# Rotary positions of the attention heads: tables with the column gains in them, quarters exchanged by transfers, and the head's sum and low part on VectorE

## The reference, cut to what matters

```python
def rope_rotate(x, ang):
    m = ang.shape[-1]
    x1, x2 = x[..., :m], x[..., m:]
    c = jnp.cos(ang)[:, None, :]
    s = jnp.sin(ang)[:, None, :]
    return jnp.concatenate([x1 * c - x2 * s, x2 * c + x1 * s], axis=-1)
...
    q = rms_norm(q.reshape(b_, s_, ATTN_HEADS, HEAD_DIM), qn_g)
    k = rms_norm(k.reshape(b_, s_, KV_HEADS, HEAD_DIM), kn_g)
    q = apply_axial_rope(q, ang_row, ang_col)
    k = apply_axial_rope(k, ang_row, ang_col)
...
        sc = jnp.einsum('bqkgd,bskd->bkgqs', qblk, k).astype(jnp.float32) * scale
        pr = jax.nn.softmax(sc, axis=-1).astype(v.dtype)
        return jnp.einsum('bkgqs,bskd->bqkgd', pr, v)
```

## Time and profile before

| what | value |
|---|---|
| median of three runs | 1665.84 us |
| the profiled execution | 1665.42 us, of which its span is 1663.6 us |
| granted TensorE clock, mean of the span | 0.993 |
| TensorE matmul busy | 1618.1 us, 97% |
| VectorE, ScalarE, GpSimd busy | 64%, 40%, 6% |
| stretch of the units above | about 851 to 1089 us of the span |

### The profile page before, as it was taken

The page is one execution under the profiler, slowest core; times in us unless marked ns, Lnnn a source line. Parts: engine busy times, 40 slices in busy tenths (PEclk is TensorE's granted clock), DMA queues, the critical chain, the costliest instruction groups (busy, mean ns, idle before and its releaser), DMA issues.

```text
span 1663.6 us, 23794 instructions
## 1 busy us (share of the span) xinstructions
PE 1618.1 (97%) x9484; PEld 1566.3 (94%) x9484; DVE 1057.5 (64%) x1628; ACT 668.9 (40%) x1073; POOL 102.2 (6%) x59
## 2 busy tenths in 40 slices
PE   5999999999999999999999999999999999999999
PEld 5999889989999999999999888788999999999998
DVE  6432665676776577477653666668767747756764
ACT  4333224453343244144332666655424414423431
POOL 4000200000000000000122322100000000000000
PEclk7999999999999999999999999999999999999999
DMA  4122002221222222212211100022122221221222
GB/s 135 51 64 63 26 14 69 59 76 50 78 76 67 61 77 78 75 51 70 83 58 39 38 21 20 9 80 64 55 73 77 73 77 54 70 80 55 77 71 81
DMA packets 193629, 103.85 MB, mean 62 GB/s; under 512 B 3792, under 2 KB 191184, under 8 KB 193520
## 3 DMA queue, kind: packets, MB, share of 16 engines
q1 hardware_dynamic: 193040, 101.20, 21.5%
q0 software_dynamic: 144, 0.79, 0.1%
q10 hardware_dynamic: 336, 0.35, 0.1%
HBM read 99.18 MB, written 3.15 MB: 62 GB/s over the span
## 4 chain that ended last, share of the span: by engine, by line
PE 92%; DVE 4%; ACT 1%; issue 1%; DMA 0%; POOL 0%; SPq 0%; ACTq 0%; DVEq 0%; POOLq 0%
PE unit_ps L536 15%; PE unit_ps L537 14%; PE unit_ps L538 14%; PE unit_ps L819 13%; PE unit_ps L817 13%; PE unit_ps L818 13%; PE unit_ps L995 2%; PE misc_ps L682 1%; PE misc_ps L536 1%; PE misc_ps L538 1%; PE misc_ps L952 1%; PE misc_ps L537 1%; PE misc_ps L963 1%; PE unit_ps L710 1%; PE misc_ps L668 1%
## 5 line engine op out<-in xcount | busy, mean ns | idle before, releaser
L817 PE MATMUL unit_ps<-h_pair,w_hi 128*128 128x384 f32 x1232 | 412.2, 335 | 3.1 <-ACT t L1297 3.0
L819 PE MATMUL unit_ps<-h_pair,w_lo 128*128 128x384 f32 x1232 | 411.6, 334 | 0.0
L818 PE MATMUL unit_ps<-h_pair,w_hi 128*128 128x384 f32 x1232 | 411.6, 334 | 0.0
L536 PE MATMUL unit_ps<-pair_b,w_hi 128*128 128x384 f32 x960 | 323.3, 337 | 6.5 <-DVE w_lo L1429 5.0
L538 PE MATMUL unit_ps<-pair_b,w_lo 128*128 128x384 f32 x960 | 320.9, 334 | 0.0
L537 PE MATMUL unit_ps<-pair_b,w_hi 128*128 128x384 f32 x960 | 320.8, 334 | 0.0
L817 PEld LDWEIGHTS unit_ps<-h_pair,w_hi 128*128 128x128 f32 x1232 | 231.2, 188 | 4.2 <-ACT t L1297 3.6
L818 PEld LDWEIGHTS unit_ps<-h_pair,w_hi 128*128 128x128 f32 x1232 | 231.3, 188 | 0.0
L819 PEld LDWEIGHTS unit_ps<-h_pair,w_lo 128*128 128x128 f32 x1232 | 231.2, 188 | 0.0
L536 PEld LDWEIGHTS unit_ps<-pair_b,w_hi 128*128 128x128 f32 x960 | 180.2, 188 | 8.9 <-DVE w_lo L1429 6.3
L537 PEld LDWEIGHTS unit_ps<-pair_b,w_hi 128*128 128x128 f32 x960 | 180.3, 188 | 0.6
(11 more groups left out here) (241 smaller groups left out, 2109.3 us busy)
## 6 DMA issues: line engine op xcount, KB each, us to landing
w_raw<-in_w_gate SPq DMA_DIRECT2D x22, 512.0 KB, 3.9
w_raw<-in_w_up SPq DMA_DIRECT2D x22, 512.0 KB, 5.2
w_raw_more<-in_w_gate SPq DMA_DIRECT2D x22, 512.0 KB, 3.9
w_raw_more<-in_w_up SPq DMA_DIRECT2D x22, 512.0 KB, 5.2
w_raw<-in_w_down SPq DMA_DIRECT2D x24, 384.0 KB, 3.5
w_raw_more<-in_w_down SPq DMA_DIRECT2D x24, 384.0 KB, 3.6
w_raw<-in_ab_w_in SPq DMA_DIRECT2D x17, 512.0 KB, 3.9
w_raw<-in_c_w_in SPq DMA_DIRECT2D x12, 512.0 KB, 3.8
```

The lines of the kernel that those rows point to most:

```text
L536: pe.matmul(out, w_hi, m_hi, start=start, stop=False)
L817: pe.matmul(out, hi, m_hi, start=starts and k == 0, stop=False, skip_group_check=True)
L818: pe.matmul(out, hi, m_lo, start=False, stop=False, skip_group_check=True)
L819: last = pe.matmul(out, lo, m_hi, start=False, stop=k == HK - 1, skip_group_check=True)
```

## The change

A head's exchange of quarters no longer runs on TensorE. The sine table carries the signs, and ScalarE scales both tables by the gains in place (`gained_ropes`, line 1351 before goes): once for the keys, and, after GpSimd has loaded the tables a second time, once for the queries, with the gains of the sine table exchanged as the quarters are. VectorE evacuates a head straight into T[2] or T[3]; ScalarE squares from there; SyncE issues four transfers per head inside the on-chip memory, 32 partitions by 768 columns each, that write T[0] as the head with its quarters exchanged (`turn_head`, placed in SyncE's order ahead of the load of the unit four later). VectorE then does T[0] times the sine table, T[4] plus T[0] (slot at+4 for a query, at+6 for a key), and the low part (`head_lo`, slot at+9). GpSimd is left with the product by the cosines. The high part moves to slot at+7. The factor 128 to the power -1/2 goes into `head_root`, and the small instruction of line 1887 goes. The table of constants is a fourth shorter, `columns` three columns longer.

```diff
-    _put(_at + (4 if _kind == "q" else 5), "turn", _i, 0)
-    _put(_at + (6 if _kind == "q" else 5), "turn", _i, 1)
-    _put(_at + 8, "split", _i)
+    if _kind == "k":
+        _put(_at + 5, "broadcast", _i)
+    _put(_at + (6 if _kind == "k" else 4), "turn", _i)
+    _put(_at + 7, "split", _i)
+    _put(_at + 9, "low", _i)
...
+            def turn_head(i):
+                sp.wait_ge(unit_read, reads(BASE["c"] + UNIT_OF[i]))
+                if i:
+                    sp.wait_ge(qk_sum, i)
+                for quarter in range(4):
+                    to, of = quarter * HD // 4, (quarter ^ 1) * HD // 4
+                    sp.dma_start(T[0][to:to + HD // 4, :], T[2 + i % 2][of:of + HD // 4, :]).then_inc(turn_landed, 16)
...
+                        if n - TURN_LOADS in UNIT_OF:
+                            turn_head(UNIT_OF.index(n - TURN_LOADS))
...
             def head_sums(i):
                 pe.wait_ge(qk_sq, i + 1)
-                if i:
-                    pe.wait_ge(rot_read, 2 * i)
+                pe.wait_ge(root_done, CHAIN["qk"] + i)
...
-            def turn(i, half):
-                pe.wait_ge(qk_gain, i + 1)
...
-                pe.matmul(misc_ps[:, bank, 0:HALF], rot, T[2 + i % 2][:, half * HALF:(half + 1) * HALF],
-                          start=True, stop=True).then_inc(rot_done, 1)
...
             def head_evacuate(i, n):
                 if i:
-                    act.wait_ge(qk_sum, i)
-                act.activation(T[1][:, :], T[0][:, :], ACT.Square).then_inc(qk_sq, 1)
-                if i >= 2:
-                    act.wait_ge(rot_done, 2 * (i - 1))
-                    act.wait_ge(qk_cos, i - 1)
-                act.activation(T[2 + i % 2][:, :], T[0][:, :], ACT.Copy, scale=cols[:, col:col + 1]).then_inc(qk_gain, 1)
+                    act.wait_ge(colsum_done, CHAIN["qk"] + i)
+                act.activation(T[1][:, :], T[2 + i % 2][:, :], ACT.Square).then_inc(qk_sq, 1)
...
+            def gained_ropes(kind, turn):
+                act.wait_ge(rope_landed, 16 * turn)
+                for part, col in enumerate((COL[kind + "n"], COL[kind + "n_turned"])):
+                    act.activation(ropes[:, part, :], ropes[:, part, :], ACT.Copy,
+                                   scale=cols[:, col:col + 1]).then_inc(rope_gained, 1)
...
+            gained_ropes("k", 1)
             for slot in range(SLOTS):
+                if slot == 8 * (UNIT_OF[KVH] + 1) - 4:
+                    gained_ropes("q", 2)
...
-                    done = dve.tensor_tensor(T[0][:, half * HALF:(half + 1) * HALF], ps, rstd[:, half, :], ALU.mult)
+                    i = UNIT_OF.index(j)
+                    if i >= 2:
+                        dve.wait_ge(qk_sq, i - 1)
+                        dve.wait_ge(qk_cos, i - 1)
+                        dve.wait_ge(turn_landed, 4 * 16 * (i - 1))
+                    done = dve.tensor_tensor(T[2 + i % 2][:, half * HALF:(half + 1) * HALF], ps, rstd[:, half, :], ALU.mult)
...
-                dve.tensor_tensor(T[1][:, tokens], misc_ps[:, bank, 0:HALF], ropes[:, 1, tokens], ALU.mult).then_inc(rot_read, 1)
+                dve.wait_ge(turn_landed, 4 * 16 * (i + 1))
+                dve.wait_ge(rope_gained, 2 if QK[i][1] == "k" else 4)
+                dve.tensor_tensor(T[0][:, :], T[0][:, :], ropes[:, 1, :], ALU.mult).then_inc(turn_scaled, 1)
+                dve.wait_ge(turn_scaled, i + 1)
+                dve.wait_ge(qk_cos, i + 1)
+                dve.tensor_tensor(T[4][:, :], T[4][:, :], T[0][:, :], ALU.add).then_inc(qk_sum, 1)
...
+            def head_lo(i):
+                dve.wait_ge(qk_hi, i + 1)
+                pair = kpair[:, QK[i][2]] if QK[i][1] == "k" else pairB[:, QK[i][2]]
+                dve.tensor_tensor(pair[:, 1, :], T[4][:, :], pair[:, 0, :].bitcast(F32), ALU.subtract).then_inc(qk_lo, 1)
...
+            load_ropes()
+            for i, (n, kind, _) in enumerate(QK):
+                if i == KVH:
+                    pool.wait_ge(qk_sum, KVH)
+                    load_ropes()
+                pool.wait_ge(unit_read, reads(BASE["c"] + n))
+                pool.wait_ge(rope_gained, 2 if kind == "k" else 4)
                 if i:
                     pool.wait_ge(qk_lo, i)
+                    pool.wait_ge(qk_hi, i)
                 pool.tensor_tensor(T[4][:, :], T[2 + i % 2][:, :], ropes[:, 0, :], ALU.mult).then_inc(qk_cos, 1)
-                pool.wait_ge(qk_cos, i + 1)
-                pool.wait_ge(rot_read, 2 * i + 2)
-                pool.tensor_tensor(T[4][:, :], T[4][:, :], T[1][:, :], ALU.add).then_inc(qk_sum, 1)
-                pool.wait_ge(qk_hi, i + 1)
-                pool.tensor_tensor(pair[:, 1, :], T[4][:, :], pair[:, 0, :].bitcast(F32), ALU.subtract).then_inc(qk_lo, 1)
```

More of the change, by code:

```diff
@@ L203 @@
 UNIT_OF = [n for n, _, _ in QK]
+TURN_LOADS = 4
 LAG = 3
@@ L999, in between @@
             def between(slot):
-                for what, i, *half in PLAN.get(slot, ()):
+                for what, i in PLAN.get(slot, ()):
                     if what == "sums":
                         head_sums(i)
[L1003 to L1006, removed]
+                    elif what == "broadcast":
+                        broadcast(CHAIN["qk"] + i)
                     elif what == "scores":
@@ L1937, in _ @@
                     elif what == "turn":
-                        turned(i, *half)
+                        turned(i)
+                    elif what == "low":
+                        head_lo(i)
                     elif what == "scores":
@@ L2008, in _tables @@
     backward = same & (i[:, None] >= i[None, :])
-    rot = np.zeros((P, P))
-    q = HD // 4
-    for half in (0, HD // 2):
-        for k in range(q):
-            rot[half + q + k, half + k] = -1.0
-            rot[half + k, half + q + k] = 1.0
-    return np.concatenate([ident, forward, backward, rot], axis=1).astype(np.float32)
+    return np.concatenate([ident, forward, backward], axis=1).astype(np.float32)
 def _rope():
@@ L2026, in _rope @@
             pos = (t // GRID_W if d < half else t % GRID_W).astype(np.float32)
-            rows.append(fn(pos * inv[d % (half // 2)]))
+            sign = -1 if fn is np.sin and d % half < half // 2 else 1
+            rows.append(sign * fn(pos * inv[d % (half // 2)]))
         out.append(np.stack(rows))
```

57 lines of the change are left out of this document (24 added, 33 removed).

## The result

| what | before | after |
|---|---|---|
| median of five runs | 1665.84 us (1665.64 to 1668.24) | 1659.54 us (1655.48 to 1660.14) |
| ratio, 95% interval | | 0.9947 (0.9932 to 0.9961) |
| the profiled execution, its span | 1665.42 us, 1663.6 | 1659.93 us, 1658.1 |
| granted clock, mean of that span | 0.993 | 0.989 |

The change makes the kernel 0.5% faster.

A forecast was written before the change was run, and what follows sets the result against it. TensorE, busy 97% of the span, was taken to bound the kernel. Gains of 2.6 + 1.8 + 0.1 + 2.9 + 0.5 + 1.3 = 9.2 us off 1665.4 gave 1656.2 us, range 1652.0 to 1661.0.

The forecast's parts named there:

- The products: TensorE loses 20 quarter products of 0.64 us each, 12.8 us, 1.28 per head, if nothing there comes to wait.
- The pair: VectorE's product by sines and sum, in slot 4 of a query's unit, take 1.86 us and start the low part 0.48 late.
- The wait it makes: TensorE's second flip waits 0.56 us for VectorE's second normalization in each steady unit, so 0.72 of 1.28 stays.
- Query 0 and query 1: Query 0 gains 1.3 plus the 0.5 wait for GpSimd's low part; query 1's wait eats 1.2 and leaves 0.1 us.
- Query 6: Its unit ends against a shorter one, so the square is late for the column sums; 0.5 us gain left.
- Query 7: Last query's unit, bound by VectorE and ScalarE: third flip waits, but a copy comes about 1.3 us earlier; gain 1.3.
- The sum: Gains over keys and queries: 2.6 + 1.8 + 0.1 + 2.9 + 0.5 + 1.3 = 9.2 us.
- Nearly all of it: Rival, 0.17: the pair costs less or a TensorE wait swallows no time; 12.8 + 0.5 off, 1652.1 us, units of 19.7.
- Longer chain: Rival, 0.17: queries 1 to 7 keep nothing as flip, maximum and square wait more; about 5 off, 1660.4 us.
- Product beside the pair: Rival, 0.07: GpSimd's product by cosines starts just ahead of VectorE's pair, which waits up to 1.8 us; 1667 to 1668.
- Late transfers: Rival, 0.05: transfers land after more than about 13 us, holding VectorE's pair and TensorE's second flip; about 1752 us at 24.8.

The follow-up runs named there:

- the version that waits nowhere: The changed kernel with the split of the next weight in slot 2 of a query's unit instead of slot 4; 1652.68 us, ratio 0.9903.

## Why the prediction was right

**The products.** No quarter product is left among the groups. For the keys, column sums to column sums of query 0 went from 42.83 to 39.99 us, 2.84 off (forecast 2.6); from query 0's to query 1's 10.95 to 9.66, 1.29 off (1.3). Nothing else was on the path there.

**The pair.** Forecast 1.86 us from a pair elsewhere, measured 1.86. The weight's low part stopped waiting for ScalarE, and the 1.0 us beside GpSimd's sum is gone, both as worked.

**The wait it makes.** Forecast 0.56 in the steady units and 1.2 in the first; by starts the flip is 0.60 and 1.21 late. The order behind the pair came out as laid out: low part, maximum, normalization, flip 0.05 later. Laid beside the unit of the version that waits nowhere, step by step, the unit of 20.41 differs from 19.75 at this place alone: 0.60 at the flip and 0.05 in the step behind it (0.41 against 0.36). Queries 2 to 5 together went from 83.98 to 81.58, 2.4 off where 2.9 was forecast: in each unit 0.04 more at the flip, the 0.05 behind it, and 0.03 that the products give less.

**Query 0 and query 1.** Query 1's sums to query 2's: 17.28 to 16.54, 0.74 off; the forecast had 0.5 (the wait for GpSimd's low part, gone) and 0.1. **Query 6:** 0.71 off, left at 0.5.

**Query 7.** The step said that the third flip would wait and that 1.3 would be gained. It is the second flip that waits, 1.31 us, as in the first unit. The gain is there all the same: in the run with eight transfers, which has no half-clock stretch in this unit, and the same wait of 1.31, column sums to values take 21.35 us (1038.98 to 1060.33) against 22.79, 1.44 off. In the profile of the changed kernel they take 23.00 (1033.52 to 1056.52), so the stretch at 1036 cost about 1.65. The term was right to 0.15; of its reasons the high part's earlier slot and the 1.0 us beside GpSimd stand, the wait it named is another flip's.

**The sum.** 7.8 off in the stage, and 9.4 with those 1.65 given back; forecast 9.2. That the two lie so near is in part luck: queries 2 to 5 came out 0.5 under the forecast, the keys, query 1, query 6 and query 7 0.1 to 0.2 over it each, and these misses cancel. By runs at equal clock 8.9 to 10.6. What the forecast could not hold is the clock: it was made against an execution at 0.993, and the median came from executions at 0.989 to 0.991. The range of 1652.0 to 1661.0 took that in only because other doubts had made it wide.

**What the prediction did not see.** It put the gain down to TensorE's products and priced the move of the sum as work for VectorE; that the normalization regains 1.0 us by it was in its working, but not what would be lost without that. The products alone are worth 6.0 to 7.5 us at equal clock. What the whole change has more than that lies in the units: 20.41 against 20.68 in the steady ones, 19.99 against 20.66 in query 6's. There the fourth flip no longer waits beside GpSimd's sum, so the sum's move has its part in it; the other parts of the change were not taken out one by one. The prediction's reading of the earlier trace rows also went wrong: the 1.2 us that TensorE waited for VectorE's normalizations were waits for normalizations held up beside GpSimd's sum, and with the other rows of that view such waits come to 2.2 us. Its sentence that shortening GpSimd's chain "is worth little by itself" holds for the steady units of the kernel before, and fails as soon as TensorE is faster.

It also took 11 to 12 us from a head's evacuation to its pair, about 9 for a key. That holds from query 2 on (12.4); for query 1 it is 8.9, for the keys and query 0 5.4, and there the four transfers, done some 4.5 us behind the first issue, were hidden with little to spare.

**The rivals.** *Nearly all of it* asks for units of 19.7 and 1652.1 us: refuted for this kernel by the waits, and reached by moving the low part of the weight. *Longer chain*, 1660.4, units of 21.0: refuted, units are 20.41; that the median lies near its time is the clock's doing. *Product beside the pair*: GpSimd's product runs at 954.12, 8.5 us ahead of the pair, and VectorE's product takes 0.95, as for nine of the ten heads. For the second key the two do meet, and VectorE's takes 1.43; TensorE shows no loss by it. Where it was made to happen for the queries, it cost 0.9 us of VectorE's idle time. *Late transfers*: four per head make nothing wait; eight cost TensorE 0.7 us, at query 0 alone.

## What to carry to other kernels

When an instruction goes from the bounding engine, ask what stands just behind its consumers on the other engines: a wait of 1 us beside GpSimd that cost nothing in the steady units became the limit once TensorE came earlier, and the part of the change that the profile seemed to ask for brought only 6.0 to 7.5 of its 12.8 us alone. Moved work belongs into the idle time that the profile shows ahead of the crowded slot (here 4.25 us, one slot away), and it can be the neighbour that moves: the weight's low part two slots earlier was worth more than moving the new pair. Two kernels 0.5% apart are compared at the same granted clock, not by medians of five, and even then a microsecond or two is open.

## What the runs showed of the hardware

TensorE's granted clock falls from 2.4 to 1.2 GHz for about 3.4 us, in some places 6.8, in the middle of a launch, one to five times in every execution profiled (the first 40 us and the very end left out). Some places come back, none is in every run. It needs no rest ahead of it: in the kernel before TensorE was busy 9.00 of 9.00 us ahead of the fall at 239. Ahead of the fall at 213 in the changed kernel it had been busy only 0.72 of the 2.00 us from 210 to 212. A stretch of 3.4 us cost 0.3 us at 350, 1.5 to 1.6 at 240 and at 1150, and about 1.65 at 1036, the one of 6.8 us 3.1. Between the best and the worst execution of one kernel lie 6 us, as much as the change brings in the medians.

VectorE's instructions with two inputs from the on-chip memory stood still where they met one of GpSimd's: 2.64 us instead of 1.22 for a low part, 1.84 instead of 0.95 for a product of 768 columns, each ending 0.8 to 1.1 us after GpSimd's.

A transfer inside the on-chip memory, 32 partitions by 768 columns (96 KB), lands in 2.1 us in the median, and in 1.9 us with half the columns. Its issue takes 0.6 us of SyncE's queue either way, so between these two sizes the count of transfers sets the time in the queue.
